# Expert layer of a two-block network: the v table read in order and summed through a weight matrix, and half of the u rows dotted on TensorE

## The reference, cut to what matters

```python
def peer(xn, wq, subkeys, u, v):
    q = (xt @ wq).reshape(T, PEER_HEADS, 2, PEER_QDIM // 2)
    s1 = jnp.einsum('thd,nd->thn', q[:, :, 0], subkeys[0])
    s2 = jnp.einsum('thd,nd->thn', q[:, :, 1], subkeys[1])
    v1, i1 = lax.top_k(s1, PEER_TOPK)
    v2, i2 = lax.top_k(s2, PEER_TOPK)
    cand = (v1[..., :, None] + v2[..., None, :]).reshape(T, PEER_HEADS, PEER_TOPK * PEER_TOPK)
    sc, ci = lax.top_k(cand, PEER_TOPK)
    e1 = jnp.take_along_axis(i1, ci // PEER_TOPK, axis=-1)
    e2 = jnp.take_along_axis(i2, ci % PEER_TOPK, axis=-1)
    idx = e1 * PEER_NKEYS + e2                      # 128 x 128 = 16384 experts
    gate = jax.nn.softmax(sc, axis=-1)
    h = jax.nn.gelu(jnp.einsum('cd,chkd->chk', xc, u[ic]))      # per chunk of 128 tokens
    return jnp.einsum('chk,chkd->cd', gc * h, v[ic])
```

## Time and profile before

| | us |
|---|---|
| median of 3 runs | 3222.41 (3220.86 to 3224.93) |
| span of the profiled execution, first to last instruction | 3220.0 |
| span from the first u row dotted to the end (1908.0 to 3220.0) | 1312 |
| TensorE busy, whole span | 2717.7 (84%) |
| VectorE busy | 1985.4 (62%) |
| GpSimd busy | 926.9 (29%) |
| ScalarE busy | 441.8 (14%) |
| HBM read | 918.35 MB |

### The profile page before, as it was taken

The page is one execution under the profiler, slowest core; times in us unless marked ns, Lnnn a source line. Parts: engine busy times, 40 slices in busy tenths (PEclk is TensorE's granted clock), DMA queues, the critical chain, the costliest instruction groups (busy, mean ns, idle before and its releaser), DMA issues.

```text
span 3220.0 us, 26360 instructions
## 1 busy us (share of the span) xinstructions
PE 2717.7 (84%) x9138; PEld 1612.9 (50%) x9138; DVE 1985.4 (62%) x3009; ACT 441.8 (14%) x1072; POOL 926.9 (29%) x713
## 2 busy tenths in 40 slices
...
GB/s 377 359 397 399 201 134 40 170 222 256 162 169 169 169 157 183 174 179 164 131 157 1 198 254 417 419 419 422 422 422 421 422 414 400 422 422 422 422 422 355
DMA packets 250245, 922.82 MB, mean 287 GB/s; under 512 B 16732, under 2 KB 44580, under 8 KB 183844
## 3 DMA queue, kind: packets, MB, share of 16 engines
...
...
HBM read 918.35 MB, written 8.44 MB: 288 GB/s over the span
## 4 chain that ended last, share of the span: by engine, by line
PE 56%; DMA 22%; DVE 11%; POOL 5%; issue 4%; ACT 2%; POOLq 0%; SPq 0%; DVEq 0%; ACTq 0%
PE ps L1505 16%; DMA arena<-in_peer_v,proj 13%; PE ps L1133 12%; PE ps L1551 8%; PE ps L1899 7%; DMA proj<-in_peer_v,proj 5%; PE ps L1749 3%; DMA arena<-in_peer_u,proj 3%; POOL proj L625 3%; DMA arena<-in_w_mod 2%; PE ps L1175 2%; PE ps L1259 1%; DVE arena L2716 1%; PE ps L1272 1%; DVE proj L2716 1%
## 5 line engine op out<-in xcount | busy, mean ns | idle before, releaser
L1899 PE MATMUL ps<-arena,gates 128*128 128x512 f32 x516 | 364.9, 872 | 368.9 <-DMA arena<-in_peer_v,proj 255.1
L1899 PE MATMUL ps<-proj,gates 128*128 128x512 f32 x992 | 449.4, 598 | 39.2 <-DMA proj<-in_peer_v,proj 38.9
L1899 PEld LDWEIGHTS ps<-arena,gates 128*128 128x128 f32 x516 | 142.0, 289 | 585.0 <-issue 455.4
L2716 DVE CUSTOM_DVE_ANT_0 proj<-proj,yT 128x2048 f32<-128x2048 f32 x128 | 291.8, 2291 | 229.5 <-DMA proj<-in_peer_u,proj 228.9
L1133 PE MATMUL ps<-ring,hT 128*128 128x512 f32 (+3 forms) x960 | 373.5, 551 | 1.8 <-DVE arena L2427 1.8
L2716 DVE CUSTOM_DVE_ANT_0 arena<-arena,yT 128x2048 f32<-128x2048 f32 x128 | 292.3, 2292 | 119.9 <-DMA arena<-in_peer_u,proj 116.4
L1899 PEld LDWEIGHTS ps<-proj,gates 128*128 128x128 f32 x992 | 184.7, 190 | 289.0 <-issue 287.8
L1133 PEld LDWEIGHTS ps<-ring,hT 128*128 128x128 f32 x960 | 180.1, 192 | 191.9 <-issue 165.6
L625 POOL DMA_INDIRECT arena<-in_peer_u,proj x128 | 200.1, 1563 | 234.2 <-PE ps L1817 119.2
L625 POOL DMA_INDIRECT proj<-in_peer_u,proj x128 | 230.0, 1797 | 100.2 <-DVE proj L2716 57.2
L1505 PE MATMUL ps<-arena,yT 128*128 128x256 f32 x1056 | 242.3, 379 | 0.0
...
## 6 DMA issues: line engine op xcount, KB each, us to landing
...
```

Source lines behind the costliest of these rows:

```text
L1899: ins = pe.matmul(ps[:, 4 * t + b, :], diag[:, j, :], row_slots[n % ROWS][:, NB * b:NB * (b + 1)], start=(h == 0 and j == 0), stop=(h == H ...
L2716: vec.tensor_tensor_reduce(slot, slot, xs[:, g // HEADS], 1.0, 0.0, ALU.mult, ALU.add, peer["h16"][:, 0, r:r + 1]).then_inc(sem(f"free{n % ...
```

## The change

The v table is no longer gathered. SP reads all of it in order, 128 tiles of 128 rows (`v_tiles`, four buffers). For each token tile a weight matrix W is built that has, for each of the 16384 experts and each token, the sum of the weights with which the token picked that expert (0 for most). It is built from one-hot products: the picks are transposed so that a pick lies in a partition (`turn_picks`); DVE compares the two halves of each expert number with 0 to 127 (`hot_sides`, two one-hot rows of 128 for 4 tokens at a time); POOL multiplies one of the two by the weight (`hot_weights`); PE multiplies the two for each token, 128 picks summed, into a 128x128 matrix of that token's weights (`spread`, four tokens per group); ACT copies the group into its place in SBUF (`spread_out`), five pieces for token tile 0 and three for tile 1. There are 32 groups per token tile: those of tile 0 are put between the u rows of steps 9 to 15, one every three rows, those of tile 1 follow the last u row. Then `sum_values` multiplies each v tile by its slice of W for both token tiles, four matmuls of 512 columns each.

The u rows are still gathered, 256 times, now one after the other into 6 row slots. Of each step's 16 rows DVE dots the eight odd ones as before; the eight even ones go to PE (`dot_row` on PE): in four chunks of four blocks, PE transposes a 128x128 block of the row against the identity into a PSUM bank (`turn_chunk`), ACT copies the chunk to SBUF (`row_out`), and PE multiplies it with the transposed input hT (`dot_chunk`), 16 blocks summed into a 128x128 product of all tokens with all gathered rows, whose diagonal holds the wanted dots. `dots_out` on DVE masks the eight diagonals of a step with the identity and sums them. The queries of heads 2 to 7 are still computed between the rows, now all inside the steps (`ASKS`). The input's scaling by its norm moves into `dots_out` for the even rows. Other edits are of storage: an iota table of 128 columns for the one of 16, tiles carved anew, semaphores shared in turn.

The diff, cut to its core:

```diff
+    PE_ROWS = tuple(range(0, TOP, 2))
+    NP = len(PE_ROWS)
+    on_pe = lambda r: r in PE_ROWS
+    chunk_of = lambda g, r: SLOTS * (NP * g + PE_ROWS.index(r))
+    uT = near_rows[2].rearrange("p (c n) -> p c n", n=NB)
+    dots_ps = ps[:, 2:4, :].rearrange("p a b -> p (a b)")[:, 0:NP * P].rearrange("p (r k) -> p r k", k=P)
...
+    ASKS = {(0, 0): ((2, 0), (2, 1)), (0, 2): ((2, 2), (2, 3)), (0, 6): ((3, 0), (3, 1)), (0, 8): ((3, 2), (3, 3))}
+    ASKS |= {(g, 2 * s + 2): ((EARLY + g - 1, s),) for g in range(1, 1 + HEADS - EARLY) for s in range(SLOTS)}
...
+    EXPERT_TILES = P
+    GROUP = 4
...
+    SPREAD_AT = {ROW(HEADS + 1, 0) + 3 * i: i for i in range(GROUPS)}
+    HOT_LAG = (4, 8)
...
+    v_tiles = (tab[:, TAB.shape[1] - D:], gates[:, 0, :], arena[:, D:2 * D], gates[:, 1, :])
+    NV = len(v_tiles)
+    AHEAD = NV - 1
+    ENDING = 4
...
-        sp.wait_ge(*at("unit_used", SLOTS * (BLK["wq"] + 4)))
-        load("norm_in", out_gain, a["final_norm_2"].partition_broadcast(P))
+        sp.wait_ge(*at("experts", GS + 1))
+        for e in range(EXPERT_TILES):
+            if e == AHEAD:
+                sp.wait_ge(*at("w_built", 2 * GROUPS))
+                load("norm_in", out_gain, a["final_norm_2"].partition_broadcast(P))
+            if e >= NV:
+                sp.wait_ge(*v_used(e - NV + 1))
+            sp.dma_start(v_tiles[e % NV], a["peer_v_2"][P * e:P * (e + 1), :]).then_inc(sem(f"slot{e % NV}"), 16)
...
+        def hot_weights(i):
+            t, j = divmod(i, GROUPS)
+            pool_eng.wait_ge(*at("pick_out", 3 if t else 1))
+            pool_eng.wait_ge(*at("hot", i + 1))
+            first = hot(i)[:, 0]
+            pool_eng.tensor_tensor(first, first, pick_T(t, 2)[:, GROUP * j:GROUP * (j + 1)].unsqueeze(2).to_broadcast([P, GROUP, P]), ALU.mult).then_inc(sem("hot_weights"), 1)
...
         for g in range(GS):
-            if g + 1 < GS:
-                pool_eng.wait_ge(*at("experts", g + 3))
             for r in range(TOP):
-                if g + 1 < GS:
-                    gather(a["peer_u_2"], g + 1, r, U_ROW(g + 1, r))
-                gather(a["peer_v_2"], g, r, V_ROW(g, r))
...
+                gather(g, r)
+                if ROW(g, r) - HOT_LAG[1] in SPREAD_AT:
+                    hot_weights(SPREAD_AT[ROW(g, r) - HOT_LAG[1]])
+        for i in range(GROUPS, 2 * GROUPS):
+            hot_weights(i)
...
+        def row_out(g, r):
+            for c in range(SLOTS):
+                q = chunk_of(g, r) + c
+                act.wait_ge(*at("u_turned", q + 1))
+                if q >= SLOTS:
+                    act.wait_ge(*at("u_dotted", q - SLOTS + 1))
+                act.copy(uT[:, q % SLOTS, :], ps[:, q % 2, :]).then_inc(sem("u_copied"), 1)
...
+        def spread_out(i):
+            t, j = divmod(i, GROUPS)
+            act.wait_ge(*at("w_built", i + 1))
+            built = ps[:, w_bank(i), :].rearrange("p (j e) -> p e j", j=GROUP)
+            for lo, n, home in W_HOME[t]:
+                ins = act.copy(home[:, :, GROUP * j:GROUP * (j + 1)], built[:, lo:lo + n, :])
+            ins.then_inc(sem("w_out"), 1)
...
+            for r in range(TOP):
+                if on_pe(r):
+                    row_out(g, r)
...
+                if ROW(g, r) - HOT_LAG[0] in SPREAD_AT:
+                    spread_out(SPREAD_AT[ROW(g, r) - HOT_LAG[0]])
+        row_gelu(GS - 1)
+        picks_out(2, 2, 3)
+        for i in range(GROUPS, 2 * GROUPS):
+            spread_out(i)
         act.activation(stat[:, 12:13], stat[:, 30:31], ACT.Sqrt)
+        last_norm(0)
...
+        def turn_chunk(g, r, c):
+            q = chunk_of(g, r) + c
+            if q >= 2:
+                pe.wait_ge(*at("u_copied", q - 1))
+            for k in range(KS):
+                f = KS * c + k
+                ins = pe.transpose(ps[:, q % 2, P * k:P * (k + 1)], row_slots[ROW(g, r) % ROWS][:, P * f:P * (f + 1)], ident)
+            ins.then_inc(sem("u_turned"), 1)
+        def dot_chunk(g, r, c):
+            t, q = g // HEADS, chunk_of(g, r) + c
+            pe.wait_ge(*at("u_copied", q + 1))
+            if (r, c) == (0, 0) and g:
+                pe.wait_ge(*at("dots_out", g))
+            for k in range(KS):
+                f = KS * c + k
+                ins = pe.matmul(dots_ps[:, PE_ROWS.index(r), :], hT[:, f, P * t:P * (t + 1)], uT[:, q % SLOTS, P * k:P * (k + 1)],
+                                start=(f == 0), stop=(f == KT - 1), skip_group_check=True)
+            ins.then_inc(sem("u_dotted"), 1)
+        def dot_row(g, r):
+            pe.wait_ge(*row_in(ROW(g, r)))
+            turn_chunk(g, r, 0)
+            for c in range(1, SLOTS):
+                turn_chunk(g, r, c)
+                dot_chunk(g, r, c - 1)
+            dot_chunk(g, r, SLOTS - 1)
...
+        def spread(i):
+            pe.wait_ge(*at("hot_weights", i + 1))
+            if i >= 2:
+                pe.wait_ge(*at("w_out", i - 1))
+            for j in range(GROUP):
+                ins = pe.matmul(ps[:, w_bank(i), P * j:P * (j + 1)], hot(i)[:, 1, j, :], hot(i)[:, 0, j, :], start=True, stop=True)
+            ins.then_inc(sem("w_built"), 1)
         for g in range(GS):
-            t, h = g // HEADS, g % HEADS
-            if g == HEADS:
-                pe.wait_ge(*at("wq_out", HEADS + 2))
-                pe.wait_ge(*at("later_out", HEADS))
-            for j, r in enumerate(by_pe(g)):
-                n = V_ROW(g, r)
-                pe.wait_ge(*at("diag_out", DIAGS[g] + j + 1))
-                pe.wait_ge(*row_in(n))
-                for b in range(2 if (g, r) == SHARED_ROW else 4):
-                    last = by_pe(g)[-1] if g < GS - 1 or b < 2 else by_pe(g)[-2]
-                    ins = pe.matmul(ps[:, 4 * t + b, :], diag[:, j, :], row_slots[n % ROWS][:, NB * b:NB * (b + 1)],
-                                    start=(h == 0 and j == 0), stop=(h == HEADS - 1 and r == last))
-                ins.then_inc(sem(f"free{n % ROWS}"), 1)
-                if 0 < g <= HEADS - EARLY and j == SCORE_AFTER:
-                    score_head(EARLY + g - 1)
-                parts = ASK_AFTER if g % 2 else ASK_AFTER_LOAD
-                if EARLY + g < HEADS and j in parts:
-                    ask_part(EARLY + g, parts[j])
+            for r in range(TOP):
+                if on_pe(r):
+                    dot_row(g, r)
+                for h, s in ASKS.get((g, r), ()):
+                    ask_part(h, s)
+                if (g, r) in SCORES:
+                    score_head(SCORES[g, r])
+                if (g, r) == (HEADS, 8):
+                    pe.wait_ge(*at("weights", HEADS))
+                    turn_picks(0, range(3))
+                if (g, r) == (GS - 1, 8):
+                    pe.wait_ge(*at("experts", GS + 1))
+                    pe.wait_ge(*at("pick_out", 1))
+                    turn_picks(1, range(2))
+                if ROW(g, r) - HOT_LAG[0] in SPREAD_AT:
...
+        def sum_values(t, e, banks):
+            pe.wait_ge(*v_in(e))
+            for b in banks:
+                ins = pe.matmul(ps[:, 4 * t + b, :], spread_weights(t, e), v_tiles[e % NV][:, NB * b:NB * (b + 1)],
+                                start=(e == 0), stop=(e == EXPERT_TILES - 1), skip_group_check=True)
+            return ins
...
+        pe.wait_ge(*at("dots_out", GS))
+        for i in range(GROUPS):
+            spread(GROUPS + i)
+            early = i - (GROUPS - SLOTS * AHEAD)
+            if early >= 0:
+                sum_values(0, early // SLOTS, (early % SLOTS,))
+        pe.wait_ge(*at("w_out", 2 * GROUPS))
+        for e in range(EXPERT_TILES - ENDING):
+            if e >= AHEAD:
+                sum_values(0, e, range(SLOTS))
+            sum_values(1, e, range(SLOTS)).then_inc(sem("unit_used"), 1)
+        for t, banks in ((0, range(SLOTS)), (1, (2, 3)), (1, (0, 1))):
+            for e in range(EXPERT_TILES - ENDING, EXPERT_TILES):
+                ins = sum_values(t, e, banks)
+            ins.then_inc(sem("values_done"), 1)
...
+        def dots_out(g):
+            t = g // HEADS
+            vec.wait_ge(*at("u_dotted", SLOTS * NP * (g + 1)))
+            link(vec.scalar_tensor_tensor(out=dots_ps, in0=dots_ps, scalar=stat[:, 6 + t:7 + t], in1=ident.unsqueeze(1).to_broadcast([P, NP, P]), op0=ALU.mult, op1=ALU.mult))
+            link(vec.tensor_reduce(peer["h16"][:, 0, 0:PE_ROWS[-1] + 1:2], dots_ps, X_AXIS, ALU.add), "dots_out")
...
+        def hot_sides(i):
+            t, j = divmod(i, GROUPS)
+            vec.wait_ge(*at("pick_out", t + 1))
+            if i >= len(hot_of):
+                vec.wait_ge(*at("w_built", i - len(hot_of) + 1))
+            wide = [P, 2, GROUP, P]
+            places = peer["pick_T"][:, 3 * t:3 * t + 2, GROUP * j:GROUP * (j + 1)].unsqueeze(3).to_broadcast(wide)
+            vec.tensor_tensor(hot(i), places, tb("iota").unsqueeze(1).unsqueeze(1).to_broadcast(wide), ALU.is_equal).then_inc(sem("hot"), 1)
...
         for g in range(GS):
-            if g + 2 < GS:
-                choose_sides(g + 2)
```

(81 more changed lines are left out.)

167 lines of the change are left out of this document (71 added, 96 removed).

## The result

The changed kernel takes 3771.93 us, the median of 4 runs (3771.54 to 3772.23), against 3222.28 before: 1.1706 times as long (95% interval 1.1689 to 1.1722). The forecast was 3790 us, with a range of 3700 to 3900. The profiled execution has a span of 3770.5 us.

What follows compares the result with a forecast made beforehand. The prediction took the kernel before as bound by DMA, a stream of 512 gathers. Start 1909.6 + u rows 916 + between 83 + v sums 871 + tail 9 = 3789, about 3790 us, range 3700 to 3900.

Steps and rivals of the forecast that it cites:

- 128 even rows: u rows on TensorE: 5.81 us each with transposes, products and one exposed wait, 744 us; bounds 682 to 833.
- 15 ends of a step: A step's first dot waits for `dots_out` on VectorE, 1.5 us left exposed each, 22 us (0 to 44).
- 32 spread groups of tile 0: Between u rows: 0.89 us of products plus 0.84 us of ScalarE copies reaching PE, 55 us (28 with copies hidden).
- between u and v: After the u rows: last `dots_out`, gelu, `weigh`, 32 groups at 2.3 us and last copies, 83 us (51 to 86).
- Products are two records: TensorE throughout: a float32 product shows as two trace records, a transpose as one; 512 columns cost 0.858 us.
- half-price rival: TensorE products: each 512-column record is a whole matmul, v sums 434 us, total 3074 us, faster; 2%.
- The bound moves from DMA to TensorE: u rows: eight even rows take PE 46.5 us a step against 39.8 of gathers; v tiles 6.9 against 2.5.
- The exposed first dot: Each even row: only the first dot waits for ScalarE's copy, 0.38 us, plus 0.10 for a group behind a wait.
- rival with the clock: u rows: many short waits make TensorE's clock fall, 10.5 us a row, 590 us more, 4380 us; 6%.
- The clock under transposes: u rows: full-clock prices hold though a third of PE's time is transposes, since the trace's clock rose under transposes.
- rival 1: u rows: TensorE's clock falls through many short waits, 10.5 us a row, 590 us more, 4380 us; 6%.
- sum of the high bounds: Whole kernel: total with every term at its high bound, given as 3908 us.

Runs made afterwards that it cites:

- experiment 5: Changed kernel with the sums over v taken from only the upper 16 bits of W and v (bfloat16, cut off): 3225.04 us, 1.0010 times the kernel before.
- experiments 1 and 2: Changed kernel with none of a step's u rows on TensorE (3659.07 us), and with four instead of eight (3622.29 us).
- Experiment 3: Changed kernel with the next even row's first chunk transposed before this row's last dot, inside a step: 3721.66 us.
- experiment 6: Changed kernel without GpSimd's multiplication of the one-hot rows by the weights for token tile 1: 3752.41 us.

## Why the prediction was right, step by step

| term | forecast | measured |
|---|---|---|
| start of the u rows | 1909.6 | 1909.65 |
| 128 even rows | 744 | 751 (5.87 each) |
| 15 ends of a step | 22 | 31 |
| queries of heads 2 to 7 | 93 | 91 (steps 1 to 4: 15.2 more each) |
| 32 spread groups of tile 0 | 55 | 38 (0.89 + 0.30 each) |
| table loads | 2 | 0 |
| between u and v | 83 | 70 (2821.3 to 2891.4) |
| sums over v | 871 | 870.1 |
| tail | 9 | 8.9 |

- *Products are two records.* Everything hung on this. The chain's 870.13 us for 1012 products (2026 records, two of them of an early sum) and experiment 5 show it; the half-price rival would have brought the time under that of before.
- *The bound moves from DMA to TensorE.* Right. PE is busy for 93% and 100% of the two parts; a smaller share of rows (experiments 1 and 2) or cheaper products (5) shortens the time.
- *The exposed first dot.* Right in its place: 0.24 us idle and about 0.3 of drain and start. I had 0.38 + 0.10. Experiment 3 takes it away in five of the seven such places of a step.
- *The end of a step* was mis-sized: forecast were 1.5 us each, for the wait alone. That part measures 1.6, but the low clock behind it makes some of them 3.2, 31 us in sum. The rival with the clock had a grain of truth here, for a few us at a time; over the u rows it stands at 0.99.
- *The spread groups* were forecast 17 us too dear: of the copies' cost, taken as 0.84 us on PE, only 0.30 reached it, since the five copies overlap and take 0.84 us together, not 1.27. Behind a group a row's first dot waits 0.54 us instead of 0.24:

```profile
2567.01 1.06 PE L2021 MATMUL ps<-gates 128*128 128x128 f32 x8
...
2569.48 1.16 PE L1996 MATMUL ps<-proj,hT 128*128 128x128 f32 x8 [0.54 <-ACT proj L1107]
```

- *Between u and v* I had taken GpSimd and VectorE in turn, 2.3 us a group. Measured is 1.98: GpSimd 2.02 beside VectorE's 1.74, which overlap.

```profile
2838.56 2.02 POOL L684 TENSOR_TENSOR vboth<-vboth,proj 128x512 f32<-128x512 f32 x1
2839.92 1.74 DVE L2898 TENSOR_TENSOR gates<-proj,tab 128x1024 f32<-128x1024 f32 x1 [0.24 <-PE ps L2021]
2840.54 3.99 POOL L684 TENSOR_TENSOR gates<-gates,proj 128x512 f32<-128x512 f32 x2
2841.90 1.74 DVE L2898 TENSOR_TENSOR vboth<-proj,tab 128x1024 f32<-128x1024 f32 x1 [0.24 <-PE ps L2021]
```

  The two slow each other (experiment 6); the earlier trace rows had shown it for GpSimd only, and its row for GpSimd alone already overlaps the VectorE row by 0.5 us. PE isn't mostly idle there, as I had it: it is busy for 26.39 of 40 us.
- *The clock under transposes.* The u rows alternate transposes with products, at 0.99. What the Trainium skill says against transposes ("TensorE: Matmul & The Clock Gate", Part 4: PE-mode transpose) cost nothing here; the u rows have at most eight transposes in a row, so they don't test transposes alone.
- *Slips that change nothing.* By its own terms rival 1 adds about 600 us, not 590, and the sum of the high bounds is 3905, not 3908.

The differences nearly cancel in the u rows (911.6 us instead of 916): ends 9 too low, spread groups 17 too high, even rows 7 too low. That is luck; that the time rises is not. The stretch between gives most of the rest, -13; together 3770.5 instead of 3789. What was not tried is the other half alone, v gathered as before with u rows on TensorE; the 113 us for the even rows are thus measured only beside v read in order.
